# Two weight stripes instead of one inside each residual loop of a decoder layer

## What is computed

```python
def rmsnorm(x, g):
    x32 = x.astype(F32)
    y = x32 * lax.rsqrt(jnp.mean(x32 * x32, axis=-1, keepdims=True) + EPS)
    return (y * g.astype(F32)).astype(x.dtype)
...
    x = x + rmsnorm(mix @ w_out, g_mix_post)
    x = x + rmsnorm(cross_attn(rmsnorm(x, g_mem_pre), mem_k, mem_v, w_mem_q, w_mem_o), g_mem_post)
    x = x + rmsnorm(sq_relu_mlp(rmsnorm(x, g_mlp_pre), w_up, w_down), g_mlp_post)
```

## Time and profile before

| | |
|---|---|
| median of 3 runs | 3286.11 us (3284.52 to 3286.77) |
| profiled execution, time | 3282.77 us |
| profiled execution, span | 3280.9 us |
| PE busy | 3152.9 us, 96% of the span |
| DVE busy | 1296.6 us, 40% |
| ACT busy | 770.3 us, 23% |
| mean granted clock of PE | 0.967 |

### The profile page before, as it was taken

One profiled execution on the slowest core, in us unless ns is written; L12 is line 12 of the kernel. 1 busy time (PEld: TensorE's weight loads), 2 busy tenths in 40 slices (PEclk: granted clock), 3 DMA queues, 4 the chain that ended last, 5 costly groups with the idle time before them and its releaser, 6 DMA issues.

```text
span 3280.9 us, 54409 instructions
## 1 busy us (share of the span) xinstructions
PE 3152.9 (96%) x22617; PEld 3058.9 (93%) x22617; DVE 1296.6 (40%) x1812; ACT 770.3 (23%) x832; POOL 165.6 (5%) x265
## 2 busy tenths in 40 slices
PE   7999999989999999899899999999999999999996
PEld 6899988988989899788799999999999999999996
DVE  6544244253355534734733233232332323323246
ACT  4311122122122223322421211212112121121221
POOL 0000010211211100000000000000000000000001
PEclk8999998999999999988999999999999999999998
DMA  5433433433555644331322222222222222222331
GB/s 173 157 106 108 145 111 99 152 123 106 186 160 159 232 146 146 84 109 39 109 90 77 79 88 77 89 77 80 86 77 89 77 83 84 77 89 77 85 139 58
DMA packets 398904, 355.04 MB, mean 108 GB/s; under 512 B 9554, under 2 KB 362052, under 8 KB 396772
## 3 DMA queue, kind: packets, MB, share of 16 engines
q1 hardware_dynamic: 377456, 269.18, 27.4%
q0 software_dynamic: 21136, 84.66, 7.5%
q10 hardware_dynamic: 228, 0.06, 0.0%
HBM read 305.63 MB, written 48.23 MB: 108 GB/s over the span
## 4 chain that ended last, share of the span: by engine, by line
PE 88%; DVE 6%; issue 3%; ACT 2%; DMA 1%; DVEq 0%; POOLq 0%; POOL 0%; ACTq 0%
PE gemm L1797 77%; PE aux L1900 2%; PE gemm L1877 1%; PE gemm L1826 1%; PE aux L1978 1%; DVE yT L1577 1%; ACT w_hi L804 1%; PE aux L2004 1%; DVE yT L1778 1%; PE aux L1954 1%; PE aux L2104 1%; DVE w_lo L1150 1%; PE aux L2090 0%; PE aux L2259 0%; PE gemm L2205 0%
## 5 line engine op out<-in xcount | busy, mean ns | idle before, releaser
L1797 PE MATMUL gemm<-act_hi,w_hi 128*128 128x288 f32 x4544 | 1004.7, 303 | 6.5 <-DVE act_lo L1586 4.1
L1797 PE MATMUL gemm<-act_lo,w_hi 128*128 128x288 f32 x4544 | 982.6, 298 | 0.0
L1797 PE MATMUL gemm<-act_hi,w_lo 128*128 128x288 f32 x4544 | 982.2, 298 | 0.0
L1797 PEld LDWEIGHTS gemm<-act_hi,w_hi 128*128 128x128 f32 x4544 | 742.5, 192 | 30.6 <-DVE act_lo L1586 13.6
L1797 PEld LDWEIGHTS gemm<-act_lo,w_hi 128*128 128x128 f32 x4544 | 743.1, 191 | 0.0
L1797 PEld LDWEIGHTS gemm<-act_hi,w_lo 128*128 128x128 f32 x4544 | 741.6, 191 | 0.0
L1150 DVE TENSOR_TENSOR w_lo<-w_raw,w_hi 128x2048 fp32r<-128x2048 f32 x216 | 494.8, 2291 | 235.2 <-ACT w_hi L804 112.5
L1797 PE MATMUL gemm<-u_hi,w_lo 128*128 128x288 f32 x2048 | 438.6, 296 | 0.0
L1797 PE MATMUL gemm<-u_hi,w_hi 128*128 128x288 f32 x2048 | 438.6, 296 | 0.0
L1797 PE MATMUL gemm<-u_lo,w_hi 128*128 128x288 f32 x2048 | 438.5, 296 | 0.0
L1797 PEld LDWEIGHTS gemm<-u_hi,w_hi 128*128 128x128 f32 x2048 | 330.2, 189 | 0.0
(11 more groups left out here) (294 smaller groups left out, 2122.9 us busy)
## 6 DMA issues: line engine op xcount, KB each, us to landing
w_raw<-in_w_mlp_up SPq DMA_DIRECT2D x64, 1024.0 KB, 6.5
w_raw<-in_w_mlp_down SPq DMA_DIRECT2D x64, 1024.0 KB, 5.4
w_raw<-in_w_in SPq DMA_DIRECT2D x56, 1024.0 KB, 5.7
w_raw<-in_w_out SPq DMA_DIRECT2D x16, 1024.0 KB, 5.4
z_scratch<-z_out SPq DMA_DIRECT2D x56, 288.0 KB, 2.1
r_zin<-z_scratch POOLq DMA_DIRECT2D x8, 1152.0 KB, 6.0
xin<-in_x_prompt POOLq DMA_DIRECT2D x8, 1024.0 KB, 6.3
d_z<-z_scratch POOLq DMA_DIRECT2D x12, 576.0 KB, 5.8
```

The costliest lines, as they stand in the source:

```text
L1797: ins = M(out[half][:, 0:TH], w[b][:, cols], x[:, k, half * TH:(half + 1) * TH], start=first and n == 0, stop=last and n == 2)
```

## The change

`first_tile` becomes `first_tiles`: for each chunk, PE multiplies the squares by ones, then the chunk of the first tile, then the same chunk of the second tile into gemm2/gemm3. The separate second tile behind the loop is gone, from the query projection and from the first MLP block alike. The wait ahead of the loop asks for both stripes' `w_lo` and for the PSUM of both tiles.

```diff
-            def first_tile(k, stripe, tile):
-
-
-                pe.wait_ge(s_wlo, stripe + 1)
-                pe.wait_ge(s_evac, tile - 1)
+            def first_tiles(k, stripe, tile):
+
+
+                pe.wait_ge(s_wlo, stripe + 2)
+                pe.wait_ge(s_evac, tile)
                 for c in range(KC):
                     pe.wait_ge(n_xsq, k * KC + c + 1)
...
                     pe.wait_ge(n_lo, k * KC + c + 1)
-                    ins = parts(stripe % 2, c, slice(c * P, (c + 1) * P), act_hi, act_lo, G[0:2], c == 0, c == KC - 1)
-                ins.then_inc(s_tile, 1)
+                    for m in range(2):
+                        ins = parts((stripe + m) % 2, c, slice(c * P, (c + 1) * P), act_hi, act_lo, G[2 * m:2 * m + 2], c == 0, c == KC - 1)
+                        if c == KC - 1:
+                            ins.then_inc(s_tile, 1)
...
-            first_tile(0, S_MQ, G_MQ)
-            for j in range(1, MH):
+            first_tiles(0, S_MQ, G_MQ)
+            for j in range(2, MH):
...
-            first_tile(1, S_MLP, G_MLP)
-            up_tile(0, 0, 1)
+            first_tiles(1, S_MLP, G_MLP)
```

## The result

The changed kernel takes 3295.05 us in the median of 10 runs (3288.82 to 3297.54), the kernel before 3285.97 (3281.93 to 3288.35): a ratio of 1.0028, with a 95% interval of 1.0018 to 1.0037. It is 9 us slower. The forecast was 3294.7 us.

A forecast was written before the change was run, and what follows sets the result against it. PE bounds nearly everywhere, but DVE bounded the two loops. Third tiles +0.2 and +4.0 us and clock +4.4 us sum to +8.6: 3291.4 us on the profiled execution, 3294.7 us on the runs' scale, range 3290.5 to 3299.0.

The forecast's parts named there:

- PE becomes the bound of the loop, at 2.565 us a chunk: Both loops: 0.80 us of added matmuls raises PE's chunk from 1.765 to 2.565 us, above DVE's 2.374.
- Rival B: Inside both loops: PE's chunk comes nearer 2.47 us, so +5.8 us in all, 3291.9 us; chance 0.12.
- rival E: Inside both loops: a chunk costs PE up to 2.78 us, so +15.0 us in all, 3301.1 us; chance 0.06.
- The last ones matmul 5.8 and 6.1 us later: End of loops 1 and 2: the slower chunks delay the start of the last ones matmul by 5.8 and 6.1 us.
- The chain T + 9.01 and T + 12.54: Behind loops 1 and 2: third stripe's `w_lo` is ready 9.01 and 12.54 us after T, the last ones matmul's start.
- +0.2 and +4.0 us for the third tiles: Behind loops 1 and 2: PE waits 6.4 and 10.0 us, so third tiles begin 0.2 and 4.0 us later.
- The clock, +4.4 us: Behind both loops: idle PE loses its clock and restarts at 0.50, costing 2.2 us each, 4.4 in all.
- The cost of nothing for what follows: Behind the third tiles: PE is the bound again and everything is only shifted by the same amount, costing nothing.
- The two rules of the Trainium skill: Bursts after long waits restart at low clock; isolated warm matmuls take 122.5 ns, making the sum 2 us smaller.
- Costs of nothing inside the loops: Waits ahead of the loop and ACT held to PE's 2.565 us cost nothing; `act_lo` comes some 3 us early.
- Rival D: Behind both loops: third stripe's `w_lo` is not last, third tile follows at once; faster, 3273.8 us; chance 0.03.
- bounds of 8.9 and 8.6 us: Loops 1 and 2: the faster outcome needs `w_lo` ready under 8.9 and 8.6 us after the last ones matmul's start.

The follow-up runs named there:

- filled: Changed kernel with 12 and 19 useless matmuls behind loops 1 and 2, keeping PE busy while it waits: 3286.58 us, ratio 1.0011 against the kernel before.
- the cut of the reciprocal: Reciprocal over 8 of 576 columns, in both kernels: changed kernel 3287.89 us (ratio 1.0009 against before), kernel before 3283.70 us (1.0001 against itself uncut).
- the first filled kernel: Changed kernel with 15 and 24 useless matmuls behind loops 1 and 2: 3292.41 us, ratio 1.0021 against the kernel before.
- the kernel with loop 2 alone: Changed kernel with loop 1 taken back to its old form: 3287.01 us, ratio 0.9982 against before; run again 3291.35 us, ratio 1.0024.
- the shortened chain: Changed kernel with the reciprocal over 8 of 576 columns: 3287.89 us, ratio 1.0009 against the kernel before.

## Why the prediction was right

The mechanism is the one forecast: the chain behind the loop's last sum, the two waits and the clock. The time, 3295.05 against 3294.7, is closer than its terms deserve. This is where the time lies in the profiles (us; "again" is the second profile of the changed kernel, "filled" the kernel with 12 and 19 matmuls; each forecast is that of the third tile plus 2.2 for the clock):

| stretch | before | changed | again | filled | forecast for the change |
|---|---|---|---|---|---|
| first ones matmul of loop 1 to the cross attention | 75.1 | 76.5 | 77.7 | 75.0 | +2.4 |
| cross attention | 149.6 | 152.5 | 150.8 | 149.6 | 0 |
| first ones matmul of loop 2 to the end | 1709.0 | 1714.1 | 1714.1 | 1712.0 | +6.2 |
| sum | 1933.6 | 1943.1 | 1942.6 | 1936.6 | +8.6 |

The places of the forecast lost 6.6 and 7.7 us, less than the 8.6, and the cross attention, which it put at nothing, 3.0 and 1.3. That the two errors cancel is luck. One by one:

- **PE becomes the bound of the loop, at 2.565 us a chunk.** Measured 2.548 (14 chunks from 1356.73 to 1392.39) in loop 1. Rival B (2.47) and rival E (2.78) are out.
- **The last ones matmul 5.8 and 6.1 us later.** Measured 5.7 and 5.6 (40.49 and 40.35 us behind the first, against 34.79 in both).
- **The chain T + 9.01 and T + 12.54.** Measured 8.90 and 12.26 to `w_lo`'s end; the third tiles begin at T + 8.95 and T + 12.40. In loop 1 the difference is in the first link: the reciprocal begins 2.09 us after T, not 2.20.
- **+0.2 and +4.0 us for the third tiles.** Measured 0.0 and +3.3.
- **The clock, +4.4 us.** Keeping it up gave back 4.8 us, with a wide spread. Behind the loops 3.1 and 2.9 us ran at 0.50 in the first profile, less than the 4.3 to 6.1 us of the rows that I took it from, and 6.2 and 2.9 in the second: 2.7 and 4.0 us. So the term is right in kind and, on these two profiles, somewhat too large.
- **The cost of nothing for what follows** ("everything is shifted by the same amount") is the step that did not hold in the profiles: the cross attention took 3.0 and 1.3 us more. Whether that belongs to the change is not shown.
- **The two rules of the Trainium skill.** By the Trainium skill, TensorE: Matmul & The Clock Gate, "HAM oscillation — how this bites in real kernels", bursts behind long waits start at the low clock: the trace agrees, with a granted clock of 0.50 behind the waits of 6.25 and 9.68 us. By "Back-to-back issue gap" of the same page of the Trainium skill a chunk would have cost 1.765 + 0.735 = 2.50 us; measured is 2.548, and the pairs of the second group start 0.26 to 0.27 us apart, as in the stream (0.267), where that figure gives 0.245.
- **Costs of nothing inside the loops.** ACT is held to PE's pace, as said, and `act_lo` is still early: the list of PE's waits has none for it in the new loops, where the kernel before had 4.1 us in 19 times.
- **Rival D, the faster outcome,** needed the third stripe not to be last. It was last in both loops; the cut of the reciprocal shows the dependence from both sides. Its bounds of 8.9 and 8.6 us are misread there: under them the third tile begins earlier than before, but to follow the loop at once the chain would have to be under the 2.57 us that the loop's matmuls last behind T.

Of the 14.1 us between the two profiled spans, 4.6 lie ahead of loop 1, where both kernels are the same (first ones matmul at 1347.33 and 1351.90); in the changed kernel's second profile it came at 1345.62. So the two profiled executions overstate the change; the medians don't.

## What to carry to other kernels

Before work is moved into an engine's gaps, ask what it covered where it stood. Here the second tile hid a chain of 9 and 12.5 us that hangs on the loop's end, and moving all of it turned a free chain into a wait and a clock loss. The right amount here was the smaller of two numbers: what the gaps hold without moving the loop's last sum, and what the chain can spare from its cover; 7 and 3 chunks of 16 gave 7 us where 16 and 16 had cost 9, and more chunks gave no more that the runs could tell. And as one link is shortened, look for the next in the same trace: here ACT's order, then a DMA queued behind stores.

## What the runs showed of the hardware

The two ones matmuls of a chunk, in float32, seemed to take 0.755 us, and the first pair behind them 0.48 instead of 0.267. The 24 fillers of the first filled kernel suggest otherwise; each stands as two in the timeline of PE:

```profile
1615.89 11.80 PE L2148 MATMUL aux<-act_hi,ones 128*128 128x288 f32 x48
1627.32 0.64 PE L1797 MATMUL gemm<-act_hi,w_hi 128*128 128x288 f32 x2
```

From 1615.89 to 1627.32 that is 0.476 us each, so two cost 0.95, which is the 0.755 and the 0.21 us by which the first pair was too long. It is a reading of sums that fit, not a test: a duration read from one start to the next can hide such a tail in the next instruction.

Behind the waits for `w_lo` the low clock lasted for quite different times, with the same stream of matmuls behind it. From the third tile's start to the rise of the clock it took 2.8, 3.1 and 6.2 us after three waits of 6.25, and 2.9, 2.9, 3.1 and 6.2 after four of 9.7. The longest of the last four, in the second run of the kernel with loop 2 alone:

```profile
1628.20:1634.20 6.00, 6.00 (x25) 6.00 (x26) 3.49 (x4) 3.17 (x3) 0.00 (x0) 0.50 0.63 175
```

After the wait of 3.60 us in the shortened chain it was 5.5, and after the 5.4 us wait in the attention stage 6.1. So the length of the wait does not tell how long the low clock lasts, and one profile does not give its price: 1.2 to 2.7 us for each such stretch here.
